# A tuned fp32 transformer kernel: who makes the first high parts and sums the first squares, and the order of TensorE's first passes

## The reference, cut to what matters

```python
def rmsnorm(x, g):
    xf = x.astype(jnp.float32)
    y = xf * lax.rsqrt(jnp.mean(xf * xf, axis=-1, keepdims=True) + EPS)
    return (y * g.astype(jnp.float32)).astype(x.dtype)

def swiglu(h, w_gate, w_up, w_down):
    return (jax.nn.silu(h @ w_gate) * (h @ w_up)) @ w_down

x = x + 0.5 * swiglu(rmsnorm(x, ffn1_norm[0]), ffn1_w_gate[0], ffn1_w_up[0], ffn1_w_down[0])
```

## Time and profile before

| what | us |
|---|---|
| median of three runs | 1677.58 |
| lowest, highest | 1676.75, 1678.23 |
| the profiled execution, its own time | 1678.01 |
| its span | 1676.2 |
| TensorE busy in the span | 1647.0 |
| VectorE, ScalarE, GpSimd busy | 1205.8, 939.4, 95.5 |

### The profile page before, as it was taken

How to read it: one execution, slowest core, us unless ns; L and a number is a source line. 1 busy time by engine, 2 the same in 40 slices (tenths; PEclk the granted TensorE clock), 3 DMA queues, 4 the chain that set the end, 5 groups by cost and what they waited for, 6 DMA issues and landing times.

```text
span 1676.2 us, 28306 instructions
## 1 busy us (share of the span) xinstructions
PE 1647.0 (98%) x10136; PEld 1458.4 (87%) x10136; DVE 1205.8 (72%) x1675; ACT 939.4 (56%) x1527; POOL 95.5 (6%) x105
## 2 busy tenths in 40 slices
PE   9999999999999999999999999999999999999998
PEld 8999997799999999998789999986888888688887
DVE  7876796558666787676876876667686668867665
ACT  5655563545555565555764655557555556755553
POOL 0100012000000010002600100000000001000000
PEclk9999999999999999999999999999999999999999
DMA  8665555355655465555415565551465553236651
GB/s 291 205 201 188 163 175 167 100 176 177 199 187 183 144 207 197 185 175 165 149 64 176 199 211 183 185 181 46 137 231 190 191 190 134 80 127 225 190 189 60
DMA packets 79040, 285.95 MB, mean 171 GB/s; under 512 B 8816, under 2 KB 9200, under 8 KB 78720
## 3 DMA queue, kind: packets, MB, share of 16 engines
q1 hardware_dynamic: 77904, 281.12, 51.3%
q0 software_dynamic: 608, 3.15, 0.6%
q10 hardware_dynamic: 464, 0.82, 0.2%
HBM read 284.00 MB, written 1.05 MB: 170 GB/s over the span
## 4 chain that ended last, share of the span: by engine, by line
PE 89%; DVE 6%; ACT 4%; issue 1%; DMA 0%; POOL 0%; POOLq 0%; ACTq 0%; DVEq 0%; SPq 0%
PE ps L2158 26%; PE ps L2162 13%; PE ps L2042 13%; PE ps L2103 6%; PE ps L2104 6%; PE ps L2105 6%; PE ps L2136 3%; PE ps L2137 3%; PE ps L2138 3%; DVE wlo L1461 1%; PE ps L2648 1%; ACT whi L973 1%; PE ps L1974 1%; DVE acts L1331 1%; PE ps L2580 1%
## 5 line engine op out<-in xcount | busy, mean ns | idle before, releaser
L1461 DVE TENSOR_TENSOR wlo<-raw,whi 128x1024 fp32r<-128x1024 f32 x380 | 461.0, 1223 | 111.5 <-ACT whi L973 111.3
L2158 PE MATMUL ps<-acts,whi 128*128 128x512 f32 x2016 | 505.7, 393 | 0.2
L973 ACT ACTIVATE whi<-raw 128x1024 fp32r<-128x1024 f32 x380 | 394.4, 1049 | 73.6 <-PE ps L2162 73.6
L2158 PEld LDWEIGHTS ps<-acts,whi 128*128 128x128 f32 x2016 | 365.3, 189 | 67.9 <-DVE wlo L1461 0.6
L2162 PEld LDWEIGHTS ps<-acts,wlo 128*128 128x128 f32 x2016 | 275.0, 190 | 19.8
L2162 PE MATMUL ps<-acts,wlo 128*128 128x256 f32 x2016 | 281.0, 282 | 0.0
L1297 DVE TENSOR_TENSOR wlo<-raw,whi 128x1024 fp32r<-128x1024 f32 x152 | 184.1, 1236 | 74.8 <-ACT whi L833 74.4
L2042 PE MATMUL ps<-whi,acts 128*128 128x512 f32 (+3 forms) x772 | 220.6, 369 | 4.8 <-ACT arena L924 3.6
L833 ACT ACTIVATE whi<-raw 128x1024 fp32r<-128x1024 f32 x152 | 155.7, 1054 | 88.1 <-PE ps L2042 35.7
L982 ACT ACTIVATE hidden<-prob 128x256 f32<-128x256 f32 x132 | 55.2, 418 | 266.7 <-DVE prob L1477 266.7
L2103 PE MATMUL ps<-hid_hi,wlo 128*128 128x256 f32 x704 | 199.2, 283 | 0.0
(11 more groups left out here) (268 smaller groups left out, 2066.8 us busy)
## 6 DMA issues: line engine op xcount, KB each, us to landing
raw<-units SPq DMA_DIRECT2D x532, 512.0 KB, 4.2
arena<-mem_in POOLq DMA_DIRECT2D x2, 1024.0 KB, 7.6
x<-x_in SPq DMA_DIRECT2D x4, 256.0 KB, 5.1
arena<-mem_in POOLq DMA_DIRECT2D x4, 256.0 KB, 5.8
out<-x SPq DMA_DIRECT2D x4, 256.0 KB, 2.1
const<-const_in ACTq DMA_DIRECT2D x1, 560.0 KB, 3.4
row<-row_in ACTq DMA_DIRECT2D x1, 134.0 KB, 3.4
gain<-gain_in ACTq DMA_DIRECT2D x1, 76.5 KB, 4.0
```

The lines of the kernel that those rows point to most:

```text
L973: nc.scalar.activation(whi[:, u % RING, :], raw[:, u % RAW, :], ACT.Copy).then_inc(hi_ready, 1)
L1461: V.tensor_tensor(wlo[:, u % RING, :], raw[:, u % RAW, :], whi[:, u % RING, :].bitcast(F32), ALU.subtract).then_inc(lo_ready, 1)
L2158: T.matmul(ps[:, bank, :], whi[:, slot, w], acts[:, k].rearrange("p e s -> p (e s)"), start=k == 0, stop=False)
```

## The change

Three things change in the first feed-forward part, all behind a test for the kernel's beginning (`self.u == 0`, `U0 == 0`, `m == 0`):

- **High parts.** ScalarE makes tiles 0, 1, 4, 5, 6, 7, VectorE tiles 2 and 3 (a multiplication by the gain's column). Two new semaphores replace `norm_hi` for these eight, so TensorE's later counts on `norm_hi` drop by 8. VectorE's list becomes: highs 2 and 3, lows 0 and 1, `wlo` 0, lows 2 to 7, `wlo` 1 to 3, `wlo` 4 and 5, chunk 0. ScalarE's becomes: highs 0 and 1, `whi` 0, highs 4 to 7, `whi` 1, square 0, `whi` 2, square 1, `whi` 3, squares 2 and 3, `whi` 4 and 5, chunk 0.
- **Squares.** GpSimd's `folded(0)` adds them up and folds, instead of VectorE's.
- **TensorE's order.** The six passes run as unit 0 high, unit 0 w_lo, unit 1 high, unit 0 low, unit 1 low, unit 1 w_lo. Unit 2 starts when its high part is there and waits for its low part in the middle.

```diff
@@ -32,6 +32,7 @@
 NB = 4
 RAW, RING, LEAD = 6, 6, 4
 DRAIN = 3
+FIRST_HI = {"act": (0, 1, 4, 5, 6, 7), "dve": (2, 3)}
 IDLE = 14
 
 BESIDE = {1: (0, 4), 2: (4, 6), 3: (6, 8)}
@@ -383,6 +384,8 @@
         rows_ready = sem("rows_ready")
         norm_hi = sem("norm_hi")
         norm_lo = sem("norm_lo")
+        first_hi_act = sem("first_hi_act")
+        first_hi_dve = sem("first_hi_dve")
         square_ready = sem("square_ready")
         fold_ready = sem("fold_ready")
         cols_done = sem("cols_done")
@@ -712,7 +715,10 @@
                     self.root(name)
 
                 def ffn(self, name, _g, _k, end, m=None, low=None):
-                    self.squares += BANKS
+                    if m == 0:
+                        self.folded(0)
+                    else:
+                        self.squares += BANKS
                     self.root(name)
                     self.spreads += 1
                     if m == 0:
@@ -888,13 +894,19 @@
                 def norm(self, name, g, k0, m=None, lowered=False):
 
                     at = GAIN_AT[g] + k0
-                    start = self.u == 0
+                    if self.u == 0:
+                        for k in FIRST_HI["act"]:
+                            self.x_tile(k)
+                            nc.scalar.activation(act_hi[:, k, :], x[:, k, :], ACT.Copy, scale=gain[:, at + k:at + k + 1]
+                                                 ).then_inc(first_hi_act, 1)
+                            if k in (1, KD - 1):
+                                self.split(1)
+                        self.bank_squares(lambda b: bank_of(x, b), self.x_here, {0: 1, 1: 1})
+                        return
                     for k in range(KD):
                         self.x_tile(k)
                         self.high(x[:, k, :], at + k, k)
-                        if start and k in (1, KD - 1):
-                            self.split(1)
-                    self.bank_squares(lambda b: bank_of(x, b), self.x_here, {1: 1, 3: 1} if start else {})
+                    self.bank_squares(lambda b: bank_of(x, b), self.x_here)
 
                 def take(self, dsts):
 
@@ -1366,12 +1378,38 @@
                 def norm(self, name, g, k0, m=None, lowered=False):
 
                     at = GAIN_AT[g] + k0
-                    start = self.u == 0
+                    if self.u == 0:
+                        self.first_norm(at)
+                        return
                     for k in range(0 if not lowered else KD, KD):
                         self.low(x[:, k, :], at + k, k)
-                        if start and k in (3, KD - 1):
-                            self.split(1)
-                    self.folded({1: 1, 3: 1} if start else {})
+                    self.folded()
+
+                def first_norm(self, at):
+
+                    def high(k):
+                        dve.wait_ge(x_landed[k // 2], 16)
+                        V.tensor_scalar(act_hi[:, k, :], x[:, k, :], gain[:, at + k:at + k + 1], None, ALU.mult
+                                        ).then_inc(first_hi_dve, 1)
+
+                    def low(k):
+                        for who, made in (("act", first_hi_act), ("dve", first_hi_dve)):
+                            if k in FIRST_HI[who]:
+                                dve.wait_ge(made, FIRST_HI[who].index(k) + 1)
+                        dve.wait_ge(x_landed[k // 2], 16)
+                        V.scalar_tensor_tensor(out=act_lo[:, k, :], in0=x[:, k, :], scalar=gain[:, at + k:at + k + 1],
+                                               in1=act_hi[:, k, :].bitcast(F32), op0=ALU.mult, op1=ALU.subtract
+                                               ).then_inc(norm_lo, 1)
+
+                    for k in FIRST_HI["dve"]:
+                        high(k)
+                    low(0)
+                    low(1)
+                    self.split(1)
+                    for k in range(2, KD):
+                        low(k)
+                    self.split(3)
+                    self.squares += BANKS
 
                 def evacuate(self, units_, dst, banks, name):
 
@@ -2012,7 +2050,7 @@
                             between[k]()
                         if fresh:
                             self.his += 1
-                            pe.wait_ge(norm_hi, self.his)
+                            pe.wait_ge(norm_hi, self.his - KD)
                         self.row_tile(kts, k, width, banks, per, fresh)
                     self.ea += 1
                     for t in range(TT):
@@ -2088,6 +2126,12 @@
                         pe.wait_ge(evac_dve, self.keys_at)
                     self.turn(turn_tiles(km, XH))
 
+                def first_ready(self, k):
+
+                    for who, made in (("act", first_hi_act), ("dve", first_hi_dve)):
+                        if k in FIRST_HI[who]:
+                            pe.wait_ge(made, FIRST_HI[who].index(k) + 1)
+
                 def idle_turns(self):
 
                     pe.wait_ge(half_ready, 2)
@@ -2152,11 +2196,13 @@
                         self.idle_turns()
                     sum_unit = self.sum_rows if end.startswith("fpost") else self.sum_unit
 
-                    def columns(slot, bank):
+                    def columns(slot, bank, low=None):
                         for k in range(KD):
                             w = slice(k * P, (k + 1) * P)
                             T.matmul(ps[:, bank, :], whi[:, slot, w], acts[:, k].rearrange("p e s -> p (e s)"),
                                      start=k == 0, stop=False)
+                        if low is not None:
+                            pe.wait_ge(lo_ready, low)
                         for k in range(KD):
                             w = slice(k * P, (k + 1) * P)
                             ins = T.matmul(ps[:, bank, 0:S], wlo[:, slot, w], act_hi[:, k, :], start=False,
@@ -2174,7 +2220,7 @@
                             for k in range(KD):
                                 w, bank = slice(k * P, (k + 1) * P), 4 + n
                                 if n == 0 and part_ != "w_lo":
-                                    pe.wait_ge(norm_hi if part_ == "hi" else norm_lo, k + 1)
+                                    self.first_ready(k) if part_ == "hi" else pe.wait_ge(norm_lo, k + 1)
                                 weights = (wlo if part_ == "w_lo" else whi)[:, slots[n], w]
                                 moving = (act_lo if part_ == "lo" else act_hi)[:, k, :]
                                 at = S if part_ == "lo" else 0
@@ -2183,12 +2229,15 @@
                             return ins
 
                         if alone:
-                            for n in range(2):
-                                pe.wait_ge(hi_ready, n + 1)
-                                whole(n, "hi", True, False)
-                                whole(n, "lo", False, False)
-                                pe.wait_ge(lo_ready, n + 1)
-                                whole(n, "w_lo", False, True).then_inc(unit_used, 1)
+                            whole(0, "hi", True, False)
+                            pe.wait_ge(lo_ready, 1)
+                            whole(0, "w_lo", False, False)
+                            pe.wait_ge(hi_ready, 2)
+                            whole(1, "hi", True, False)
+                            whole(0, "lo", False, True).then_inc(unit_used, 1)
+                            whole(1, "lo", False, False)
+                            pe.wait_ge(lo_ready, 2)
+                            whole(1, "w_lo", False, True).then_inc(unit_used, 1)
                             self.his += KD
                             return
 
@@ -2203,7 +2252,7 @@
 
                         for hi in (True, False):
                             for k in range(KD):
-                                pe.wait_ge(norm_hi if hi else norm_lo, his + k + 1)
+                                pe.wait_ge(*((norm_hi, his - KD + k + 1) if hi else (norm_lo, his + k + 1)))
                                 for n in range(2):
                                     ins = part(n, k, hi)
                                     if not hi and k == KD - 1:
@@ -2232,7 +2281,11 @@
                     first_chunk()
                     if name == "fpre0":
                         self.evacuated()
-                    gate(1, U0 + 2, 0)
+                    if U0 == 0:
+                        pe.wait_ge(hi_ready, 3)
+                        columns(2, 6, 3)
+                    else:
+                        gate(1, U0 + 2, 0)
                     self.columns_of_fold(0, 0)
                     up(1, U0 + 3, 0)
                     self.spread(0)
```

## The result

The changed kernel takes 1683.41 us (median of seven, 1682.27 to 1684.18) against 1677.58 (1676.47 to 1678.23): the ratio is 1.0034, with a 95% interval of 1.0024 to 1.0044. It is slower by 5.8 us, where 1679.7 was forecast with a range to 1682.0. The two profiled executions are 1684.18 and 1678.01 us, spans 1682.4 and 1676.2, so 6.2 us lie between the traces. The seven times of the kernel before lie in two groups, 1676.5 to 1676.8 and 1677.6 to 1678.2 us, and its profiled execution is one of the later group.

A forecast was written before the change was run, and what follows sets the result against it. TensorE, busy 98% of the span, was taken as the bound. Order of passes -0.7, no wait before the spread -0.3 and wait for the fold +3.1 gave +2.1 us, so 1679.7 us, range 1677.0 to 1682.0.

The forecast's parts named there:

- ScalarE gained nothing from its two highs: First passes: ScalarE saves 0.8 us on two highs but waits for transfers, so from `whi` 1 on it stands where it stood.
- The order of the passes: First six passes on TensorE: the new order ends them at 14.24 instead of 14.94 us, 0.7 us won.
- The neighbours at the port: GpSimd's adds and VectorE's `wlo` block each other in strict turns, 1.12 and 1.08 us each, so the fold comes at 20.06.
- the wait for the fold: After unit 2's `columns`, TensorE idles from 17.0 to 20.1 us until GpSimd's fold is there: +3.1 us.
- Then by turns: add 1 to 13.95: GpSimd's first add gets the turn right behind `wlo` 1 (ending 12.83) and ends at 13.95, ahead of `wlo` 2.
- the clock stays: Behind TensorE's 3.1 us wait for the fold, the granted clock stays at 1.00, in the case forecast given 60%.
- this rival: The clock falls in the 3.1 us gap from 17 us: 2.6 us more, 1682.3 us; chance 17%.
- The price of 2.6 us: Cost if the clock falls: TensorE's work in 5.2 us behind the gap goes at half speed.
- The undisturbed GpSimd: Rival: no turns form at the port, the fold is there at 17.55, `gate(2)` 0.4 us sooner, 1677.2 us; chance 15%.
- The late turns: Rival: GpSimd gets in only after `wlo` 5, fold at 22.8, `gate(2)` 4.8 us later, 1682.4 us; chance 5%.
- the clock's case: The rival in which the clock falls in TensorE's new gap, priced at 1682.3 us; chance 17%.

The follow-up runs named there:

- e7: The kernel before with the shared high parts alone (VectorE makes tiles 2 and 3), squares and TensorE's order as before; 1677.35 us against 1676.69, ratio 1.0005.
- e2: The kernel before with only GpSimd adding up and folding the first squares, highs and TensorE's order as before; 1679.35 us against 1677.26, ratio 1.0014.
- e1: The changed kernel with the first squares summed and folded by VectorE again, shared highs and new order kept; 1678.44 us against 1677.90, ratio 1.0005.
- e8: The changed kernel with VectorE waiting for the fold between `wlo` 2 and `wlo` 3; 1680.73 us against 1677.90, ratio 1.0018.
- e10: The changed kernel with one 32-column memset in VectorE's list between `wlo` 2 and `wlo` 3; 1683.36 us, ratio 1.0035 against the kernel before.
- e3: The kernel before with TensorE's new order of the passes alone; 1677.86 us against 1677.26, ratio 1.0002.
- e5: The changed kernel with one 128x128 add on GpSimd behind its memsets, into an unread tile; 1683.42 us, ratio 1.0036 against the kernel before.
- e9: The changed kernel with GpSimd's first add made to wait for the end of `wlo` 1; 1683.77 us, ratio 1.0038 against the kernel before.
- e4: The changed kernel with 16 unread matmul turns on TensorE between unit 2 and the fold's columns; 1681.13 us against 1677.90, ratio 1.0022.
- e6: The kernel before with TensorE's new order, and VectorE's means, chunk 0's add and diagonal ahead of `wlo` 5; 1676.82 us against 1677.26, ratio 0.9997.

## Why the prediction was wrong

**What held.** ScalarE gained nothing from its two highs: `whi` 1 starts at 9.35 instead of 9.32 (e7 shows the waits for transfers). The order of the passes won what was worked out: unit 2 at 14.28, forecast 14.24. The neighbours at the port were the right mechanism, with 1.12 and 1.08 us a turn. e2 alone moved the time to 1.0014, e1 without it to 1.0005. The Trainium skill, "SBUF — State Buffer", section "Summary: rules for kernel authors", says of this pair that the second one to issue fully blocks until the first finishes. The traces agree that one blocks the other: 2.06 us beside `wlo`, 1.29 without (e8). They don't agree on the order: the first add was issued at 12.57 us, ahead of `wlo` 2 (12.80) and `wlo` 3, and both passed it.

**The term that was mis-sized: the wait for the fold, 4.43 instead of 3.1 us.** The failing step is "Then by turns: add 1 to 13.95". The first add lost the two turns of `wlo` 2 and `wlo` 3 and ended at 16.32. One more `wlo` thus came ahead of the fold than I had counted (five, where my sum has four: 1.08 us), and the fold itself had nothing left to overlap (0.80 instead of 0.63 us from the third add's end). It was there at 21.52 instead of 20.06, the rest being hundredths of each turn. The row it came from, at 817 us, had only one `wlo` in front of it.

**The step that failed: the clock stays.** I gave its fall 17% because 2.3 us without matmuls at 815 us had not moved the granted clock, and because "no stretch of this trace shows such a fall". Both readings fail. The second is false: in the trace of the kernel before the granted clock falls at 330.5 us, in the second of two waits of 1.37 and 1.68 us, and stays at 0.50 for 6.8 us. And the first row was one draw. All twelve traces (before, after, e1 to e10) have that same wait of 2.3 us; behind it, or at its end, the clock fell in eight of them (after, e1, e2, e3, e5, e7, e9, e10) and stayed in four (before, e4, e6, e8). Here the second wait near 330 us and the clock behind it, before, and then the stretch behind the wait of 2.3 us in e3:

```profile
331.61 1.09 PE L2636 MATMUL ps<-const,prob 128*128 128x128 f32 x4 [1.68 <-DVE prob L1922]
...
332.00:333.00 1.00, 1.00 (x6) 0.91 (x5) 0.88 (x4) 0.27 (x1) 0.00 (x0) 0.50 0.03 8
```

```profile
817.00:818.00 1.00, 1.00 (x4) 0.67 (x3) 1.00 (x2) 0.00 (x0) 1.00 (x1) 0.50 0.97 369
```

At the beginning the clock fell in all six traces with an unfilled wait of 1.64 us or more (after, e2, e5, e8, e9, e10). With the fold at the forecast's 20.06 TensorE would have idled 3.1 us, so this rival was the likeliest course once the turns were granted. e4 shows its share: filling the gap brings back 2.3 us of time and 2.8 us in the trace (3.56 instead of 6.34).

The price of 2.6 us against 2.70 measured in the trace is in part luck: the clock was low for 6.8 us, not 5.2, but the first 0.7 us of that passed before TensorE had work. The 5.2 us came from the weight loads of 333 ns at the start. The granted clock reads 1.00 in every window from 1 to 6 us there, so only their duration speaks for the lower level; the same turns in e4, at 1.00, take 192 ns.

The forecast with these two put right is 1679.7 + 1.5 + 2.7 = 1683.9 us; 1683.4 was measured. The Trainium skill, "TensorE: Matmul & The Clock Gate", section "Why this matters for your kernels", warns that idle gaps between bursts of matmuls take the clock back to half. The traces agree, and here shorter gaps than the one in the earlier trace rows did it (1.64 us in e2).

**The other rivals.** The undisturbed GpSimd (1677.2) fell with the 2.06 us adds. The late turns (5%: GpSimd only behind `wlo` 5) came half true: not all, but two turns were lost. The range ended at 1682.0, below even the clock's case at its own price (1682.3), and no case had the longer wait and the clock together.

**What stays open.** Why an unbroken row of two-input instructions keeps the port, and why being held up once ends this, isn't explained; e10 shows only that a break of one small instruction is enough. Why the pair at 817 us took turns from the first is open too. What decides whether the clock falls behind a given wait isn't shown: it is not the length of the wait alone, since behind the same 2.3 us it fell in eight traces and stayed in four.

## What to carry to other kernels

Work moved from VectorE to GpSimd beside a row of VectorE instructions with two SBUF inputs isn't moved off VectorE's time: add up all of both until the result that someone waits for, and look at whether the row has a break, before you count the first turn. A wait of TensorE can have a second price, the work behind it at half clock, which here was 1.5 us for a wait of 1.64 and 2.7 for one of 4.43. A trace in which such a gap did no harm is no bound, not even for the same gap in the next execution. Look through the whole trace for low granted clocks, and at other traces of the same stretch, before you price one. And a gain ahead of a join (0.7 us of better order) is worth nothing until the other arm, here the diagonal on VectorE, comes sooner too.

## What the runs showed of the hardware that I had not expected

- Three `wlo` in an unbroken row take 3.50 us with GpSimd's add waiting since 12.57 us; with a 32-column memset between the second and third the add ends 1.0 us sooner (e10). After that they alternate, 1.12 and 1.08 us a turn.
- The granted clock fell to 0.50 behind 1.64 us of idle TensorE (e2), and in the second of two waits of 1.74 and 0.74 us (e8). It was low for about 3.4 us in both (20.7 to 24.1 and 19.7 to 23.1 us), and for 6.8 us (20.8 to 27.7) in the changed kernel.
- Behind one and the same wait of 2.3 us (near 815 us before) it fell in eight of the twelve traces. In or behind the pair of waits of 1.4 and 1.7 us near 330 us it fell in eleven, all but e7's.
